# A hybrid decoder layer: experts with at most 128 rows get a loop of their own

## The reference, cut to what matters

```python
_, idx = lax.top_k(jnp.where(expert_mask, sel, -jnp.inf), TOP_K)   # 8 of 64 experts for each token
gates = scores[idx] / sum * ROUTED_SCALE
for each expert e:                      # its rows are the tokens that chose it
    y = (silu(x2[rows] @ w_gate[e]) * (x2[rows] @ w_up[e])) @ w_down[e]     # 1024 -> 256 -> 1024
    acc[rows] += y * gate[rows]
out = layer_norm(alpha * x2 + acc + shared(x2))
```

## Time and profile before

| | |
|---|---|
| time, median of 3 runs | 2231.73 us (2226.25 to 2231.98) |
| span of the profiled execution | 2228.0 us |
| expert loop in it | 1236.8 to 2187.1 us, 66 turns |
| mean of a turn | 950.3 / 66 = 14.40 us |

### The profile page before, as it was taken

The page is one execution under the profiler, slowest core; times in us unless marked ns, Lnnn a source line. Parts: engine busy times, 40 slices in busy tenths (PEclk is TensorE's granted clock), DMA queues, the critical chain, the costliest instruction groups (busy, mean ns, idle before and its releaser), DMA issues. The chain is left out here.

```text
span 2228.0 us, 40720 instructions
## 1 busy us (share of the span) xinstructions
PE 2108.7 (95%) x13609; PEld 1827.3 (82%) x13609; DVE 1142.7 (51%) x3371; ACT 799.7 (36%) x1568; POOL 606.9 (27%) x1023
## 2 busy tenths in 40 slices
PE   8889999999999899998999899999999999999992
PEld 7768889888988778886877788888888988888882
DVE  5834664565465532234566555454555554555544
ACT  4223452454344421114440333333333333333334
POOL 7056654000023100001002233333333333333331
PEclk9999999999999999999999999999999999999996
DMA  4422122112334221103424999999999999999995
GB/s 157 122 52 67 44 82 81 58 44 64 91 109 138 57 76 52 43 19 110 147 76 168 305 307 305 309 314 310 303 314 307 307 307 311 315 316 312 305 293 174
DMA packets 195937, 405.06 MB, mean 182 GB/s; under 512 B 26350, under 2 KB 124742, under 8 KB 178710
## 3 DMA queue, kind: packets, MB, share of 16 engines
q1 hardware_dynamic: 164016, 317.52, 40.1%
q0 software_dynamic: 31680, 86.52, 18.2%
q10 hardware_dynamic: 166, 0.05, 0.0%
HBM read 335.79 MB, written 70.35 MB: 182 GB/s over the span
## 5 line engine op out<-in xcount | busy, mean ns | idle before, releaser
L2518 PE MATMUL ps_gu<-xe,w_raw 128*128 128x160 f32 x4224 | 592.0, 301 | 0.0
L2518 PEld LDWEIGHTS ps_gu<-xe,w_raw 128*128 128x128 f32 x4224 | 577.8, 191 | 0.2
L2557 ACT ACTIVATE w_hi<-w_raw 128x1024 fp32r<-128x1024 f32 x132 | 132.3, 1049 | 293.3 <-DMA w_raw<-in_exp_w_down 288.7
L2482 POOL DMA_INDIRECT scr_acc<-y_rest,out_idx x66 | 106.3, 1610 | 470.6 <-ACT y_rest L2577 470.6
L2601 DVE TENSOR_TENSOR w_lo<-w_raw,w_hi 128x1024 fp32r<-128x1024 f32 x132 | 155.8, 1221 | 147.3 <-ACT w_hi L2557 147.3
L1129 ACT ACTIVATE w_raw_first<-w_raw_first,o_stage 128x128 f32<-128x128 f32 (+1 forms) x192 | 86.3, 450 | 200.3 <-DVE o_stage L1077 199.4
L2482 POOL DMA_INDIRECT scr_acc<-y_main,out_idx x66 | 105.1, 1593 | 98.5 <-ACT y_main L2580 96.1
L2580 ACT ACTIVATE y_main<-ps_ye,gate 128x512 f32<-128x512 f32 x132 | 90.9, 688 | 113.2 <-PE ps_ye L84 112.1
L1808 DVE TENSOR_TENSOR e_idx_f<-ps_xt,e_neg_slot 128x2 f32<-128x2 f32 x64 | 10.2, 160 | 218.2 <-PE ps_xt L1799 218.1
L1789 DVE TENSOR_SCALAR e_sel<-e_slots,e_place 128x256 bf16<-128x256 bf16 x536 | 110.5, 280 | 0.0
L82 PE MATMUL ps_ye<-w_hi,e_h_hi 128*128 128x512 f32 x264 | 110.5, 418 | 0.0
(11 more groups left out here) (435 smaller groups left out, 4906.1 us busy)
## 6 DMA issues: line engine op xcount, KB each, us to landing
w_raw<-in_exp_w_gate SPq DMA_DIRECT2D x66, 1024.0 KB, 8.0
w_raw<-in_exp_w_up SPq DMA_DIRECT2D x66, 1024.0 KB
w_raw<-in_exp_w_down SPq DMA_DIRECT2D x66, 1024.0 KB
w_raw_first<-in_w_in SPq DMA_DIRECT2D x24, 512.0 KB, 4.4
v_w_raw<-in_w_in SPq DMA_DIRECT2D x48, 256.0 KB, 2.9
merged<-in_x SPq DMA_DIRECT2D x14, 512.0 KB, 4.7
scr_att<-o_stage SPq DMA_DIRECT2D x16, 264.0 KB, 3.0
att_prev<-scr_att SPq DMA_DIRECT2D x16, 264.0 KB
```

What stands on the lines that cost most here:

```text
L2482: pool.indirect_dma_start(out=acc_rows[c], out_offset=bass.IndirectOffsetOnAxis(ap=out_idx[j][:, c:c + 1], axis=0), in_=y[:, :], in_offset ...
L2518: ins = pe.matmul(ps_gu[:, 2 * w + c, 0:CAP], w3(raw[j][w])[:, k, P * c:P * c + P], xT[:, k, :], start=(k == 0), stop=(k == KD - 1))
L2557: act.activation(piece_of(hi[j], piece), piece_of(raw[j][DOWN], piece), ACT.Copy).then_inc(hi_made, 1)
```

## The change

The table now puts the experts with at most 128 rows first. If their number is odd or less than 2, a slot more or less is evened out so that the first loop has whole pairs. Two counts are made on the chip: `few` pairs of such items and `more` pairs of the others. Each engine has two loops in place of one, and the last pair stands behind them as before. With this input `few` is 14 and `more` is 18, so 28 turns run in the first loop, 36 in the second, and 2 behind it: 66 as before.

In a turn of the first loop

- gate, up, Silu and `h` have 128 columns in place of 160,
- the rest matmuls of the down weights, `y_rest` and its scatter are gone,
- the load of the down weights doesn't wait for rest matmuls.

The gather of the rest rows and their two transposes stay in all turns. Empty places have their indices past the 1024 tokens; the gather now has a bound there, and leaves rows past it out (`bounds_check`), in both loops. Scatters of rest rows have semaphores of their own.

```diff
@@ gather
-        for c, x in enumerate((self.x_main[j], self.x_rest[j])):
-            pool.indirect_dma_start(out=x, out_offset=None, in_=self.x_rows[c],
-                                    in_offset=bass.IndirectOffsetOnAxis(ap=self.idx[j][:, c:c + 1], axis=0)).then_inc(self.gathered[j], 16)
+        pool.indirect_dma_start(out=self.x_main[j], out_offset=None, in_=self.x_rows[0],
+                                in_offset=bass.IndirectOffsetOnAxis(ap=self.idx[j][:, 0:1], axis=0)).then_inc(self.gathered[j], 16)
+        pool.indirect_dma_start(out=self.x_rest[j], out_offset=None, in_=self.x_rows[1],
+                                in_offset=bass.IndirectOffsetOnAxis(ap=self.idx[j][:, 1:2], axis=0),
+                                bounds_check=4 * L - 1, oob_is_err=False).then_inc(self.gathered[j], 16)
@@ project_and_route, VectorE
+                ch(ts(cnt[:, 2:3], cnt[:, 0:1], P + 0.5, 0.0, ALU.is_lt, ALU.add))
...
+                n_extra, n_few = ps_cnt[:, 8:9], ps_cnt[:, 9:10]
+                ch.do(ts(room, n_few, 2.0, 0.0, ALU.max, ALU.add))
...
+                ch(ts(it.loops[0:1, 0:1], small[0:1, 4:5], 1.0, 0.0, ALU.max, ALU.add))
+                ch(dve.tensor_copy(it.loops[0:1, 1:2], small[0:1, 3:4]))
+                ch(ts(onehot[:, 0, :], slot_n[0:NE, :], first[:, 0:1], None, ALU.is_equal))
@@ experts, every engine
+        def counts(eng):
+            more = eng.value_load(it.loops[0:1, 0:1], min_val=1, max_val=57)
+            few = eng.value_load(it.loops[0:1, 1:2], min_val=1, max_val=NE // 2)
+            return few, more
@@ SyncE
                         if w == DOWN:
-                            sp.wait_ge(lo_made, 2 * (n - 2) + 2)
-                            sp.wait_ge(y_done, 3 * (n - 2) + 1)
+                            if full is not None:
+                                sp.wait_ge(rest_done, rest_free)
+                            sp.wait_ge(lo_made, free[w])
@@ GpSimd
+                    if full is not None:
+                        hold(rest_out[1 - j], 16 * (full + j))
+                        hold(rest_evac, 2 * full + j + 1)
+                        pool.indirect_dma_start(out=acc_rows[1], ... in_=y_rest[j][:, :], ... compute_op=ALU.add).then_inc(rest_out[j], 16)
@@ TensorE
+                    width = P if full is None else CAP
...
-                                ins = pe.matmul(ps_gu[:, 2 * w + c, 0:CAP], w3(raw[j][w])[:, k, P * c:P * c + P], xT[:, k, :],
+                                ins = pe.matmul(ps_gu[:, 2 * w + c, 0:width], w3(raw[j][w])[:, k, P * c:P * c + P], xT[:, k, 0:width],
...
+                    if full is not None:
+                        pe.wait_ge(h_ready, 2 * n + 2)
+                        pe.wait_ge(ld[j][DOWN], 16 * (pair + 1))
+                        pe.wait_ge(rest_evac, 2 * full + j)
...
-                with pe.Fori(0, loops) as i:
-                    for j in range(2):
-                        turn(2 * i + j, j, True, True, i)
-                turn(2 * loops, 0, True, False, loops)
-                turn(2 * loops + 1, 1, False, False, loops)
+                with pe.Fori(0, few) as i:
+                    for j in range(2):
+                        turn(2 * i + j, j, None, True, True, i)
+                with pe.Fori(0, more) as i:
+                    for j in range(2):
+                        turn(2 * (few + i) + j, j, i, True, True, few + i)
+                turn(2 * (few + more), 0, more, True, False, few + more)
+                turn(2 * (few + more) + 1, 1, more, False, False, few + more)
```

More of the change, by code:

```diff
@@ L2112, in _ @@
                     cols = slice(P * n, P * n + P)
[L2113 to L2116, removed]
+                    for j in range(NX + 1):
+                        ins = pe.matmul(ps_tab[:, cols], ecol[:, :] if w is None else base_w[:, j, :], onehot[:, j, :],
+                                        start=(j == 0), stop=(j == NX))
                 ins.then_inc(tab_done, 1)
@@ L2472, in hold, with turn @@
                     it.hold(pool, sem, value)
-                def turn(n, j, ahead1, ahead2, pair):
+                def turn(n, j, full, ahead2, pair):
                     if ahead2:
@@ L2478, in turn @@
                         it.gather(pool, n + 2, j)
-                    hold(scattered[1 - j], 32 * (pair + j))
-                    for c, y in ((1, y_rest[j]), (0, y_main[j])):
-                        hold(y_evac, 3 * n + (1 if c else 3))
-                        pool.indirect_dma_start(out=acc_rows[c], out_offset=bass.IndirectOffsetOnAxis(ap=out_idx[j][:, c:c + 1], axis=0),
-                                                in_=y[:, :], in_offset=None, compute_op=ALU.add).then_inc(scattered[j], 16)
+                    hold(scattered[1 - j], 16 * (pair + j))
@@ L2485, in _ @@
                 for s in range(4):
                     hold(it.acc_out[s], 32)
-                loops = pool.value_load(it.loops[0:1, 0:1], min_val=NE // 2 - 1, max_val=57)
-                with pool.Fori(0, loops) as i:
+                few, more = counts(pool)
+                with pool.Fori(0, few) as i:
                     for j in range(2):
-                        turn(2 * i + j, j, True, True, i)
-                turn(2 * loops, 0, True, False, loops)
-                turn(2 * loops + 1, 1, False, False, loops)
+                        turn(2 * i + j, j, None, True, i)
@@ L2493, in _ @@
+                with pool.Fori(0, more) as i:
+                    for j in range(2):
+                        turn(2 * (few + i) + j, j, i, True, few + i)
+                turn(2 * (few + more), 0, more, False, few + more)
+                turn(2 * (few + more) + 1, 1, more, False, few + more)
                 for j in range(2):
-                    pool.wait_ge(scattered[j], 32 * (loops + 1))
+                    pool.wait_ge(scattered[j], 16 * (few + more + 1))
+                    pool.wait_ge(rest_out[j], 16 * more + 16)
@@ L2506, in turn_rows, with turn @@
                     ins.then_inc(turned, 1)
-                def turn(n, j, ahead1, ahead2, pair):
+                def turn(n, j, full, ahead1, ahead2, pair):
+                    width = P if full is None else CAP
                     pe.wait_ge(x_by_act, 2 * n + 2)
@@ L2584, in _ @@
                 split_hi(0, 1)
-                loops = act.value_load(it.loops[0:1, 0:1], min_val=NE // 2 - 1, max_val=57)
-                with act.Fori(0, loops) as i:
+                few, more = counts(act)
+                with act.Fori(0, few) as i:
                     for j in range(2):
-                        turn(2 * i + j, j, True, True, i)
-                turn(2 * loops, 0, True, False, loops)
-                turn(2 * loops + 1, 1, False, False, loops)
+                        turn(2 * i + j, j, None, True, i)
+                with act.Fori(0, more) as i:
+                    for j in range(2):
+                        turn(2 * (few + i) + j, j, i, True, few + i)
+                turn(2 * (few + more), 0, more, True, few + more)
+                turn(2 * (few + more) + 1, 1, more, False, few + more)
                 norm.statistics(act)
@@ L2640, in _ @@
                 split_lo(0, 0)
-                loops = dve.value_load(it.loops[0:1, 0:1], min_val=NE // 2 - 1, max_val=57)
-                with dve.Fori(0, loops) as i:
+                few, more = counts(dve)
+                with dve.Fori(0, few) as i:
                     chi.loop(i, 14)
                     for j in range(2):
-                        turn(2 * i + j, j, True, True, i)
-                chi.end_loop(loops)
-                turn(2 * loops, 0, True, False, loops)
-                turn(2 * loops + 1, 1, False, False, loops)
+                        turn(2 * i + j, j, None, True, True, i)
+                chi.next_loop()
+                with dve.Fori(0, more) as i:
+                    chi.loop(few + i, 14)
+                    for j in range(2):
+                        turn(2 * (few + i) + j, j, i, True, True, few + i)
+                chi.end_loop(few + more)
+                turn(2 * (few + more), 0, more, True, False, few + more)
+                turn(2 * (few + more) + 1, 1, more, False, False, few + more)
                 norm.apply(dve)
```

128 lines of the change are left out of this document (77 added, 51 removed).

## The result

The changed kernel takes 2211.48 us (median of 4 runs, 2205.06 to 2217.3), the kernel before 2229.72 in the same comparison: a ratio of 0.9918, 95% interval 0.9901 to 0.9936. That is 18 us faster where 64 were forecast, and outside the range on its slow side. The profiled execution has a span of 2215.6 us. It was the slowest of the four runs (2217.3), so what is read from it is some 6 us worse than the median.

The account below looks back on a forecast made before the run. TensorE was taken as the bound, transfers 1.1 us behind. Gains of 63.6 us in first-loop turns and 2.6 in full turns, less 2 for two loops, made 64: 2231.7 to 2168 us, range 2147 to 2193 for 8 in 10.

Parts of the forecast that it names:

- TensorE, 11.4 us a few turn: First-loop turn on TensorE: 14.23 us less 1.00 for rest matmuls and 1.77 for fewer columns, giving 11.4.
- Transfers, between 11.4 and 12.8, 12.1 taken: First-loop turn: TensorE's 11.4 us from below, DMA time of 14.0 less 1.2 from above; 12.1 taken, gaining 63.6 us.
- The slack of 1.1 us: Loop of the kernel before: the down weights' low part could have ended 1.1 us later, so transfers follow TensorE that closely.
- The down load is issued right behind the up load ... I put it at nothing: First loop: the down load, no longer waiting some 2 us more, queues earlier but adds no bandwidth; gain put at nothing.
- The clock: TensorE's granted clock: forecast wrong altogether if short stalls lowered it, which 15 stalls of up to 0.8 us had not.
- `few` was 14: Count of first-loop pairs: 28 turns were assumed there, and the forecast would be wrong altogether if it weren't 14.
- 4.9 forecast: Queue q0, gathers and scatters, in the first loop: should fall from 6.1 to 4.9 us of DMA time a turn.
- 2.6 us for full turns: Second-loop turns, 38 counted: the gather skips empty rest places, saving half of 5.3 us of stalls, 2.6 us (0 to 5).
- Table and loops: Building the table: cost 0, being covered by TensorE's other work; entering two loops instead of one: cost 2 us (0 to 5).
- Rival 1: First loop: TensorE stays the bound, as weights fill weak slices and transfers need under 11.4 us; 2148 us, chance 21%.
- Rivals 2 and 3: First loop: transfers give up only their share, 2187 to 2196 us, 13%; or weight load sets the pace, 2198 us, 5%.
- Rival 4: Bounded gather makes GpSimd late: 8.6 us more eats the gain, 10 more gives some 2320 us; 3% with others slower.

Follow-up runs that it names:

- silu_first: Changed kernel, with ScalarE and VectorE splitting the next down weights behind the work this turn needs: 2149.55 us, ratio 0.9640 to the kernel before.
- down_first: Changed kernel, with SyncE loading the down weights ahead of gate and up in the first loop: 2154.59 us, ratio 0.9668 to the kernel before.
- silu_plain: silu_first, with the first loop's scatter of y_main writing its rows instead of adding them: 2150.3 us.

## Why the prediction was wrong

- *TensorE, 11.4 us a few turn.* Right in kind. In silu_first it is 11.70. The rest matmuls were 1.00 and measured 0.99. The columns were put at 1.8 and gave 1.54, since a record with 128 columns takes 113 ns and not 110. That is the term that was too large, by 0.2 us; the sum itself, 14.23 - 1.00 - 1.77, is 11.46, which was written as 11.4.
- *Transfers, between 11.4 and 12.8, 12.1 taken.* **This step failed.** 12.8 was called the bound from above, and the few turn took 14.03. It had been worked out as bytes and shares, what 16 engines need for a turn's work. The DMA share of 0.89 in the first loop seems to say that this was about right: 0.89 x 14.03 = 12.5 us. But silu_first moved the same transfers with 1.01 x 11.70 = 11.8, so the share times the turn is no fixed need. And it bounds the turn only if no single transfer has a date of its own. The down weights have one. With the rows of before: a down load goes out at 1640.58, 3.1 us ahead of the next turn's start at 1643.72. Split and both Silu must end before the transposes, 8.77 us into that turn; they take 2.0 and 0.48. So the load had 3.1 + 8.8 - 2.5 = 9.4 us, and needed 8.2 on the median. In the change it goes out 3.7 us ahead (1343.91 to 1347.60), but the transposes come at 7.2 us and the split with the Silus takes 2.4, so it has 3.7 + 7.2 - 2.4 = 8.5, and needs 9.9 on the median. The shorter matmuls, the gain itself, moved the date 1.5 us forward. (That is an estimate from one turn each; the waits above are what was lost.)
- *The slack of 1.1 us.* It was worked out for `h_lo` on VectorE alone. That ScalarE's Silu stands in the same place, and that the transposes wait for it, was not looked at. `h_lo` was expected to cost 0.7 us in most few turns. It cost 15.1 us in 16 waits, about that size each but in half of the turns, and the Silu 24.3 us in 14 waits beside it.
- *"The down load is issued right behind the up load ... I put it at nothing".* It was issued 2 us sooner, but behind a whole up load: its first packet came 5.1 us after the issue and not 2.3, and the split began 9.9 us after it and not 8.2. down_first shows what the place of that load is worth: 57 us.
- *The clock.* That short stalls might lower it was named as what would make the forecast wrong. Stalls of up to 0.8 us had not done it, nor had the one turn of before with 1.1 and 0.8. In the change the clock stood at 0.50 eight times in the first loop: four times at a Silu stall of 3.6 to 4.0 us, and four times in turns with stalls of 1.3 to 1.9 us alone; other turns with stalls of 1.3 us kept 1.00. The 320 us of the stage view hold 22.8 turns of 14.03; at silu_first's 11.70 their work is 267 us, and TensorE was busy for 288. So of 53 us lost there 32 are idle, and 21 are work that took longer. The clock was at 0.50 for 37.5 of the 320 us and TensorE busy for 33.0 of these, which at full clock would be 16.5, if all of it scales with the clock: that much is the clock, and the last 4 or 5 us are not accounted for.
- *The rest.* `few` was 14; q0 fell to 33.5% of the first loop (1240 to 1620 us), 4.7 us a turn against 4.9 forecast. Of the 2.6 us for full turns nothing came (14.34 both times). Table and loops can't be told from zero. Rival 1 has the place where the kernel lands once the order is repaired (2148 against 2149.55), in part by luck: the few turns give 75 us there and the full ones 5, where its terms were 83 and 2.6, less 2 for the loops. Rivals 2 and 3 gave times nearer to the result (2187 to 2198), but for causes that no run bears out: the transfers fit in 11.7 us, and the matmuls did follow their columns. Rival 4 is refuted, as the bound costs 0.08 us. Three slips of the working change nothing: rival 1's 84 needs 2.97 us a turn and not the 2.9 written (with 11.46 as the turn it is 82); the longest small operation is 0.27 us, not 0.25; and of slices 8 to 19 of the earlier trace rows only those to 13 lie before the issue of the gate load, which comes 4.8 us into the turn.

What stays open: of the 2.3 us lost in a few turn about half goes with the adding scatter. The packets show that the down load now stands behind the up load for 2.8 us more, and down_first, which takes that away, wins all of it back. But how the 2.3 us divide between the place behind the up load and the earlier date is not shown: the up load was not moved by itself.

## What to carry to other kernels

Where an engine and the transfers are both full, the share of busy time gives no ceiling for the turn, and only a rough floor (12.5 us by it here, where 11.7 was reached). For the ceiling take each load that stands at the head of an in-order queue, its time from issue to landing, and the date by which what is queued behind it is needed; a shorter turn moves that date forward. In ScalarE's queue the Silu, ready for microseconds, started at 1358.43, with the end of the split. The Trainium skill, TensorE: Matmul & The Clock Gate, section Architectural detail: the array is 16× 32×32, not 1× 128×128, gives ScalarE and VectorE strict first-in first-out queues; the trace agrees with that start. So put work on prefetched data behind the work of the present turn, on every engine of the chain at once. A total of waits is no price: ScalarE waited 288.7 us for down weights in the loop before, where the order cost 11 us, and 275.6 in the change, where it cost 62.

## What the runs showed of the hardware

An adding scatter takes about twice the DMA time of the same bytes written or loaded. The DMA view of the changed kernel while almost only the scatter runs, 1341 to 1342 us, and while almost only weights flow, 1361 to 1363 us:

```profile
DMA packets 51, 0.21 MB, mean 209 GB/s; under 512 B 0, under 2 KB 0, under 8 KB 51
...
DMA packets 203, 0.83 MB, mean 416 GB/s; under 512 B 10, under 2 KB 10, under 8 KB 193
```

With a plain scatter q0's share in silu_plain was 24.0% for the bytes that took 36.4%, gathers included. Packet by packet, close to half of q0's 4 KB packets took about 327 ns in the first loop of silu_first and as many 159; in silu_plain over nine in ten took 159. And a bound on an indirect gather doesn't make GpSimd dearer by more than the 0.08 us above.
